# First loads of a two-block transformer kernel on one DMA queue, in another order

## The reference

```python
cond = jax.nn.silu(c)                      # 1024 numbers
mod = cond @ w_ada[l] + b_ada[l]           # 9 x 1024 numbers: sh1, sc1, gt1, sh2, ...
u = modulate(rmsnorm(h, g_norm_ffn1[l]), sh1, sc1)   # h is x: rmsnorm(x)*g*(1+sc1)+sh1
h = h + 0.5 * gt1 * swiglu(u, w_ffn1_in[l], w_ffn1_out[l])
```

## Time and profile before

| what | us |
|---|---|
| median of 3 runs (1117.57 to 1119.99) | 1118.47 |
| the profiled execution's own time | 1117.76 |
| its span in the profile | 1116.0 |
| PE busy in the span | 1077.0 (97%) |
| DVE busy | 874.7 (78%) |
| ACT busy | 633.1 (57%) |
| first matmul of the first chunk starts | 43.35 |

### The profile page before, as it was taken

How to read it: one execution, slowest core, us unless ns; L and a number is a source line. 1 busy time by engine, 2 the same in 40 slices (tenths; PEclk the granted TensorE clock), 3 DMA queues, 4 the chain that set the end, 5 groups by cost and what they waited for, 6 DMA issues and landing times.

```text
span 1116.0 us, 24969 instructions
## 1 busy us (share of the span) xinstructions
PE 1077.0 (97%) x10736; PEld 819.0 (73%) x10736; DVE 874.7 (78%) x1130; ACT 633.1 (57%) x792; POOL 90.5 (8%) x104
## 2 busy tenths in 40 slices
PE   6999999999999999999999999999999999999996
PEld 5677777688788577777778785877758877597773
DVE  4789699788787885554667967999966886799994
ACT  1544344463466554444367555877755755687771
POOL 1114621043000110000000000000000000000000
PEclk9899999999999999999999999999999999999998
DMA  9999799754556578554546226499993523579981
GB/s 340 370 371 373 278 316 359 247 177 160 189 187 229 195 254 305 194 184 167 175 143 237 94 77 231 184 378 416 414 315 107 183 89 108 222 263 396 416 363 39
DMA packets 134717, 271.94 MB, mean 244 GB/s; under 512 B 9428, under 2 KB 98104, under 8 KB 126296
## 3 DMA queue, kind: packets, MB, share of 16 engines
q1 hardware_dynamic: 124248, 231.79, 58.1%
q0 software_dynamic: 7904, 29.25, 7.3%
q10 hardware_dynamic: 2464, 9.44, 2.2%
HBM read 269.41 MB, written 1.05 MB: 242 GB/s over the span
## 4 chain that ended last, share of the span: by engine, by line
PE 81%; DVE 10%; ACT 4%; DMA 3%; issue 2%; ACTq 0%; DVEq 0%; SPq 0%
PE ps L750 67%; PE ps L1625 3%; DVE wlo L469 3%; DMA area<-in_w_ada_dram 2%; PE ps L1673 1%; PE ps L892 1%; PE ps L902 1%; DVE area L2841 1%; PE ps L910 1%; PE ps L1278 1%; PE ps L1247 1%; PE ps L1087 1%; DVE bnst L2282 1%; ACT area L1776 1%; PE ps L1308 1%
## 5 line engine op out<-in xcount | busy, mean ns | idle before, releaser
L469 DVE SCALAR_TENSOR_TENSOR wlo<-raw,whi 128x2048 f16<-128x2048 f32 (+4 forms) x212 | 466.0, 2231 | 36.6 <-ACT whi L444 36.0
L444 ACT ACTIVATE whi<-raw 128x2048 f16<-128x2048 f32 (+4 forms) x212 | 385.2, 1850 | 25.8 <-DMA raw<-in_w_ffn_in_dram 10.2
L750 PE MATMUL ps<-uhi,whi 128*128 128x256 f16 (+2 forms) x1328 | 329.6, 260 | 2.2 <-DVE ulo L2308 2.0
L750 PE MATMUL ps<-uhi,wlo 128*128 128x256 f16 (+2 forms) x1328 | 329.4, 260 | 0.0
L750 PE MATMUL ps<-ulo,whi 128*128 128x256 f16 (+2 forms) x1328 | 329.4, 260 | 0.0
L750 PE MATMUL ps<-whi,hreg 128*128 128x512 f16 (+1 forms) x656 | 205.0, 381 | 0.0
L750 PE MATMUL ps<-area,whi 128*128 128x96 f16 (+2 forms) x2168 | 155.0, 210 | 0.0
L750 PEld LDWEIGHTS ps<-area,whi 128*128 128x128 f16 (+2 forms) x2168 | 145.4, 99 | 11.7 <-issue 5.6
L750 PE MATMUL ps<-area,wlo 128*128 128x96 f16 (+2 forms) x1084 | 149.4, 210 | 0.0
L750 PEld LDWEIGHTS ps<-uhi,whi 128*128 128x128 f16 (+1 forms) x1328 | 130.3, 98 | 23.5 <-issue 8.9
L750 PEld LDWEIGHTS ps<-ulo,whi 128*128 128x128 f16 (+1 forms) x1328 | 130.2, 98 | 15.6 <-issue 1.9
(11 more groups left out here) (358 smaller groups left out, 1324.6 us busy)
## 6 DMA issues: line engine op xcount, KB each, us to landing
raw<-in_exp_w_gate_up_dram SPq DMA_DIRECT2D x64, 1024.0 KB, 8.4
raw<-in_w_ffn_in_dram SPq DMA_DIRECT2D x44, 1024.0 KB, 7.5
raw<-in_w_in_dram SPq DMA_DIRECT2D x34, 1024.0 KB, 7.0
area<-in_w_ada_dram POOLq DMA_DIRECT2D x48, 512.0 KB, 7.1
raw<-in_w_ffn_out_dram SPq DMA_DIRECT2D x22, 1024.0 KB, 7.6
raw<-in_exp_w_down_dram SPq DMA_DIRECT2D x22, 1024.0 KB, 9.2
raw<-in_w_out_dram SPq DMA_DIRECT2D x12, 1024.0 KB, 4.9
x<-in_exp_w_down_dram SPq DMA_DIRECT2D x6, 1024.0 KB, 10.1
```

Source lines behind the costliest of these rows:

```text
L444: act.activation(whi[:, u.slot, 0:n], raw[:, u.slot, 0:n], ACT.Copy, scale=SW)\
L469: dve.scalar_tensor_tensor(out=wlo[:, u.slot, 0:n], in0=raw[:, u.slot, 0:n], scalar=SW, in1=whi[:, u.slot, 0:n], op0=ALU.mult, op1=ALU.sub ...
L750: last = pe.matmul(o, st, mv, start=start and i == 0, stop=stop and i == 2, skip_group_check=True)
```

## The change

Three things move. ACT's queue now carries, after `x`: the first three scale pieces, unit 0, the last scale piece, unit 1. SP no longer issues units 0 and 1 of this layer; after its constants it waits as before for the shift sums and PE's shift piece, and in addition for the landing of the third scale piece, and then goes on with unit 2. DVE makes the low part of unit 0 between the sums of the third and of the last scale piece, no longer behind both.

```diff
-        def ada_first(eng, b):
+        def ada_first(eng, b, js):
-            for j in (0, 3, 1, 2):
+            for j in js:
                 eng.dma_start(first_w[b][j], w_ada[:, 2 * j:2 * j + 2, b * D:(b + 1) * D]).then_inc(ada_in[b][j], 16)
+        def fetch(eng, u, src):
+            k, n = src.shape[1], src.shape[2]
+            eng.dma_start(raw[:, u.slot, 0:k * n].rearrange("p (k n) -> p k n", k=k), src).then_inc(raw_in[u.slot], 16)
...
             def phase(ph):
-                load(Unit(ph.u0), ph.src("a", 0))
-                load(Unit(ph.u0 + 1), ph.src("b", 0))
                 if ph is ffn1:
                     sp.wait_ge(ada_sum, 6)
                     sp.wait_ge(ada_pe, 1)
+                    sp.wait_ge(ada_in[1][1], 16)
+                else:
+                    load(Unit(ph.u0), ph.src("a", 0))
+                    load(Unit(ph.u0 + 1), ph.src("b", 0))
...
-            ada_first(act, 0)
+            ada_first(act, 0, (0, 3, 1, 2))
...
-            ada_first(act, 1)
+            ada_first(act, 1, (0, 3, 1))
+            act.wait_ge(lo_made, Unit(ffn1.u0).count(1 - RING))
+            fetch(act, Unit(ffn1.u0), ffn1.src("a", 0))
+            ada_first(act, 1, (2,))
+            act.wait_ge(lo_made, Unit(ffn1.u0 + 1).count(1 - RING))
+            fetch(act, Unit(ffn1.u0 + 1), ffn1.src("b", 0))
             act.wait_ge(used, RING)
             act.wait_ge(stack_in, 16 * 20)
             rms_first()
...
             ada_first_sums(1, (0, HALF, D), range(2))
             rms_xn(0)
-            ada_first_sums(1, (0, HALF, D), range(2, 6))
+            ada_first_sums(1, (0, HALF, D), range(2, 4))
             lo_part(dve, Unit(0))
+            ada_first_sums(1, (0, HALF, D), range(4, 6))
```

More of the change, by code:

```diff
@@ L559, in load @@
                 sp.wait_ge(lo_made, u.count(1 - RING))
-                k, n = src.shape[1], src.shape[2]
-                sp.dma_start(raw[:, u.slot, 0:k * n].rearrange("p (k n) -> p k n", k=k), src).then_inc(raw_in[u.slot], 16)
+                fetch(sp, u, src)
             sp.dma_start(cstack[0:8, :], a["c"][0].rearrange("(r n) -> r n", n=P)).then_inc(const_in, 16)
```

## The result

The changed kernel takes 1120.43 us in the median of 20 runs (1119.03 to 1122.75), the kernel before 1118.07 us (1113.38 to 1120.04) in 20 runs beside it. The ratio is 1.0029, with a 95% interval of 1.0020 to 1.0038: slower, by 2.4 us in the medians and 3.2 us by the ratio. In the profiled executions the span is 1118.4 against 1116.0 us, +2.4. The forecast was 1123.7 us by the same mechanism (+5.2 on the 1118.47 that it started from); the direction and the mechanism were right, the size was about twice what came.

A forecast was written before the change was run, and what follows sets the result against it. The prediction took the start's chain through the last scale piece as the bound, with x's strand 0.87 us behind it. Opening matmuls 4.5 later, +1.8 clock gap, -1.1 later fall: +5.2 on 1118.47, 1123.7 us; 8-in-10 range 1118.3 to 1127.2.

The forecast's parts named there:

- An issue is held by its queue's backlog of packets: ACT's load issues: each waits until its queue's backlog falls to a limit between 1281 and 1442 packets.
- I take 27.3 us in place of 19.36: ACT's first square of x, behind unit 1's issue, starts at 27.3 us, the middle of 26.6 to 28.0.
- the bracket: Limit on packets ahead in ACT's queue, 1281 to 1442; unit 1's issue done when 2062 to 2223 packets have moved.
- Root, tile, transposes: ACT to DVE to PE: second root at 31.4 us, second tile 32.4, transposes end 33.4, sums of the scale 40.8.
- The clock in the gap, +1.8: PE idle 4.8 us ahead of its transposes: clock falls, costing 1.8 us, within bounds of 0 to 3.4.
- The later fall, -1.1: PE's clock fall at 39.2 us, cost 3.4 before, may come again or not; a third counted back, -1.1 us.
- DVE keeps up: DVE's sums of the last scale piece end at 40.1 (40.5) us, before PE asks for them at 40.8.
- SP's hold at nothing: SP holding unit 2 until the third scale piece lands costs nothing, covered by PE's late start.
- So whatever the change adds ahead of the first chunk is added to the end: First chunk's matmuls on PE follow each other without a wait from 43.55 us, so earlier delay reaches the end.
- ACT is not held: Rival: limit counts bytes or loads, x's strand stays, DVE's order decides: +0.6, 1119.0 us; chance 0.23.
- ACT is held longer: Rival: ACT held until most of unit 0 has moved, free at 31.0 us: 1127.4 us; chance 0.12.
- The start gets shorter: Rival: low part off the path to the columns (-0.77), loads in at 32.0 instead of 34.06: -2.8, 1115.7 us; chance 0.09.

The follow-up runs named there:

- the wide rows: Changed kernel, but ACT's load for unit 0 brings the same 1 MB in 4 KB rows instead of 1 KB rows: 1118.60 us, ratio 1.0012 to the kernel before.
- the squares first: Changed kernel with ACT's squares of x and roots ahead of its issues of unit 0, last scale piece and unit 1: 1117.76 us, ratio 1.0006 to the kernel before.
- the filled gap: Changed kernel with 22 warm-up matmuls in place of 12 ahead of PE's transposes: 1118.43 us, ratio 1.0017 to the kernel before.
- the run with the hold alone: Kernel before, with SP waiting for the third scale piece before it issues units 0 and 1; ACT and DVE as before: 1117.36 us, ratio 1.0004.
- the version that was to beat both: Kernel before plus SP's hold of units 0 and 1, second scale piece ahead of PE's transposes, 7 warm-up matmuls, scale columns before DVE's low part: 1121.61 us, ratio 1.0039.

## Why the prediction was right, and where its size was off

- *An issue is held by its queue's backlog of packets*: right. Two experiments show it, the wide rows by the count and the squares first by the order. The Trainium skill, DMA: Bandwidth & Descriptors, section "Issuing engines are not separate DMA queues", which has the cost of issuing as usually small beside the transfer, is not what this trace shows for an issue behind a full queue: 12.07 us for one issue, and 2.63 us when the megabyte ahead of it is in 4 KB rows. Three of ACT's four scale pieces before were short, so "usually" may stand; the full queue is the exception.
- *"I take 27.3 us in place of 19.36"* is the term that was mis-sized: ACT was free at 25.3. Packets of ACT's queue from the start to the end of unit 0's, of the last piece's and of unit 1's issue:

```profile
q10 hardware_dynamic: 930, 3.61, 77.8%
...
q10 hardware_dynamic: 2006, 7.70, 82.1%
...
q10 hardware_dynamic: 2079, 7.99, 82.8%
```

  Unit 0's issue ended with 2192 - 930 = 1262 packets still ahead of it, the last piece's with 3232 - 2006 = 1226, about the 1281 worked out from the earlier trace rows. Unit 1's was not held at all (0.67 us), with 3504 - 2079 = 1425 left, near the upper end of the bracket (1442). So it was the last piece's issue that set ACT free, and not unit 1's, as the prediction had it. The upper end meant 2062 packets moved, which the prediction placed at 26.6 us, counting from the landing of `x` as if no packet of a later load had moved by then, and at 284 packets in 3 us. But 1454 had moved by 19.4, not 1376, and 2079 by 25.2: 625 packets in 5.8 us, or 323 in 3 us. So both the middle of the bracket (0.7 us) and the clock time of its end (1.4 us) were taken too late. The 284 were not of the queue alone: 142 more packets moved in that stretch. Nor did one queue in place of two cost rate: from 21 to 24 us ACT's queue alone moved 418 GB/s in the changed kernel, where both together moved 414 before.
- *Root, tile, transposes*: right, shifted. The second tile is made at 30.46 instead of 32.4; the sums start 10.0 us later than that, where the prediction had 8.4 and put the clock's price apart.
- *The clock in the gap, +1.8*: right that it falls; that the size fits is partly luck. PE waited 1.99 us where 4.8 was expected, because the first tile came 1.9 us sooner than forecast and the warm-up matmuls ended 1.0 us later. The clock fell all the same: the transposes and the pass behind them lost 1.6 us (10.0 against 8.4, and the same 1.6 in the sums of the filled gap). That is half of the 3.3 us at 1.2 GHz, and not the price of twelve warm-up matmuls, from which the prediction took its 1.8 between bounds of 0 and 3.4.
- *The later fall, -1.1*: the right sign, too small. The fall came again, but for 3.4 us instead of 6.8 and later; the rows give -1.1 - 0.8 = -1.9.
- *DVE keeps up*: right, with 2.6 us to spare instead of 0.7. *SP's hold at nothing*: right, ratio 1.0004 in the run with the hold alone (there it holds units 0 and 1 too), and 1.0006 with the squares first, where the hold, the single queue and DVE's order all stay.
- *"So whatever the change adds ahead of the first chunk is added to the end"*: right for this change (+2.4 at the first silu product, at the last one and at the end). It does not hold the other way round: of the 2.4 us that SP's hold takes out ahead of the first chunk, 0.8 are left at the last silu product, and of the 2.3 us of the version that was to beat both, none.
- The sum again with the measured terms: 4.5 - 2.0 (ACT) + 1.6 (gap) - 1.9 (second fall) = 2.2, against 2.4 in the spans; the remaining 0.2 us were not taken apart. Besides the gap, two signs in the prediction were missed because ACT was free sooner: the first chunk started at 46.55 and not at 47 to 50, and unit 1's issue ended at 25.2 and not at 26 to 28.
- The rival "ACT is not held" is refuted by the row of 12.07 us, and "ACT is held longer" by ACT being free at 25.3 us and not at 31.0. "The start gets shorter" came true only in kernels without the hold, and there it brought nothing that the times show (1.0004 and 1.0039).

Open: the exact rule of the hold. Six held issues of the two kernels and the wide rows ended, counted the same way, with 1226 to 1335 packets ahead, and two with 1415 (squares first, 0.75 us) and 1425 ahead (0.67 us) were short, so it isn't one number for the whole queue. Also open is how much the late units alone cost in the version that was to beat both: that they keep the silu products where they were is read from the traces, and no run moves them by themselves. And the length of a fall of the clock is open. A wait of 1.58 us ahead of the sums was followed by 6.8 us at 1.2 GHz, one of 1.57 us by 10.2, and one of 0.87 us, in the kernel before, by 6.8: the wait alone doesn't give it.

## What to carry to other kernels

Before a load joins the queue of an engine that also computes, count the packets ahead of it, rows and not bytes, and put it behind the work that the engine could do meanwhile: a load behind a full queue arrives no sooner for being issued early. A start that gets shorter pays only as far as the loads and engines that feed PE later come earlier too; look for the first place where PE will stand and wait before spending work on it. Two late strands that meet at one wait are not added; undo one alone and the other one shows.

## What the runs showed of the hardware

- An issue on ACT's queue took 12.07 us with 1 KB rows ahead, 2.63 with 4 KB rows, 0.73 when it was made 11 us later.
- A wait of PE of 1.99 us ahead of the transposes was followed by 3.3 us at 1.2 GHz, one of 3.92 us there went with 3.4 us; waits of 1.58, 1.57 and 4.32 us ahead of the sums were followed by 6.8, 10.2 and 13.7 us.
- ACT's queue alone moved 418 GB/s (4 KB rows, changed kernel, 21 to 24 us); ACT's and SP's together 414 in the same stretch before.
- A version whose first chunk starts 2.3 us earlier was slower by 0.39%; its trace has a wait of PE of 2.73 us some 155 us later, and 6.9 us more at 1.2 GHz behind it.
